# Regrouping the slots of expert weights, moving side loads out of a mixture's head, and waiting for down weights by halves

## The reference

```
def moe_ffn(h, router_w, router_bias, w_gate, w_up, w_down):
    scores = softmax(h @ router_w)                  # 256 tokens, 16 experts
    e_idx = the two best experts of the best of four groups, by scores + router_bias
    wts = scores at e_idx, divided by their sum
    out[token] = sum over its two experts e of
                 wts * ((silu(x @ w_gate[e]) * (x @ w_up[e])) @ w_down[e])

x = layer_norm_2(ALPHA * x + g1 * y, ln_g[i, 0], ln_b[i, 0])
f = moe_ffn(x * (1 + sc2) + sh2, router_w, router_bias, exp_w_gate[i], exp_w_up[i], exp_w_down[i])
x = layer_norm_2(ALPHA * x + g2 * f, ln_g[i, 1], ln_b[i, 1])
```

## Time and profile before

| | |
|---|---|
| Median of 3 runs | 2413.11 us (2412.06 to 2414.28) |
| Span of the profiled execution | 2412.0 us |
| TensorE matmuls busy | 2288.5 us, 95% |
| VectorE busy | 1005.7 us, 42% |
| ScalarE busy | 345.9 us, 14% |
| SP's DMA queue | 691.5 MB, 73.1% of 16 DMA engines |
| Longest chain, by engine | PE 72%, DMA 14%, SP's queue 9%, VectorE 3% |

### The profile page before, as it was taken

One profiled execution on the slowest core, in us unless ns is written; L12 is line 12 of the kernel. 1 busy time (PEld: TensorE's weight loads), 2 busy tenths in 40 slices (PEclk: granted clock), 3 DMA queues, 4 the chain that ended last, 5 costly groups with the idle time before them and its releaser, 6 DMA issues.

```text
span 2412.0 us, 26071 instructions
## 1 busy us (share of the span) xinstructions
PE 2288.5 (95%) x10504; PEld 1393.8 (58%) x10504; DVE 1005.7 (42%) x2156; ACT 345.9 (14%) x705; POOL 54.5 (2%) x98
## 2 busy tenths in 40 slices
PE   6999999999999999999999999888899999998887
PEld 5888698458887785476554443333397544433333
DVE  5265656768666567124643211111235522111112
ACT  2221111001220110011531111111100011111111
POOL 0100000002000000000000000000000000000000
PEclk9999999999999999999999999999999999999999
DMA  9745968856467687532059999999944399999996
GB/s 321 261 174 197 331 229 302 315 195 227 147 255 289 241 300 293 204 115 67 36 215 383 423 421 424 424 423 422 410 172 174 125 388 421 423 424 424 424 421 274
DMA packets 181444, 706.31 MB, mean 293 GB/s; under 512 B 9296, under 2 KB 18768, under 8 KB 153424
## 3 DMA queue, kind: packets, MB, share of 16 engines
q1 hardware_dynamic: 176656, 691.50, 73.1%
q0 software_dynamic: 4672, 13.14, 1.6%
HBM read 699.33 MB, written 5.28 MB: 292 GB/s over the span
## 4 chain that ended last, share of the span: by engine, by line
PE 72%; DMA 14%; SPq 9%; DVE 3%; ACT 1%; issue 1%; DVEq 0%; ACTq 0%
PE banks L624 70%; DMA ring<-in_exp_w_up_dram 6%; DMA acc<-in_exp_w_down_dram 3%; DMA ring<-in_exp_w_down_dram 3%; SPq L2630 3%; SPq L2634 2%; SPq L2663 2%; SPq L2632 2%; DMA arena<-in_exp_w_down_dram 1%; DMA ring<-in_w_ada_dram 1%; DVE acc L1826 0%; PE banks L686 0%; DVE acc L1799 0%; ACT arena L1651 0%; ACT UT L1459 0%
## 5 line engine op out<-in xcount | busy, mean ns | idle before, releaser
L624 PE MATMUL banks<-ring,arena 128*64 128x512 f32 (+2 forms) x2624 | 718.7, 589 | 41.2 <-DMA ring<-in_exp_w_up_dram 21.4
L624 PE MATMUL banks<-UT,ring 128*128 128x256 f32 (+1 forms) x3696 | 728.6, 356 | 8.9 <-ACT UT L1459 4.3
L624 PEld LDWEIGHTS banks<-UT,ring 128*128 128x128 f32 x3696 | 623.7, 193 | 87.0 <-issue 13.6
L624 PEld LDWEIGHTS banks<-ring,arena 128*64 128x64 f32 (+1 forms) x2624 | 290.1, 151 | 439.3 <-issue 406.0
L624 PE MATMUL banks<-arena 128*64 128x512 f32 (+5 forms) x1220 | 239.0, 493 | 13.3 <-DMA acc<-in_exp_w_down_dram 5.6
L1826 DVE SCALAR_TENSOR_TENSOR acc<-ring,cact,acc 128x512 f32<-128x512 f32 x280 | 212.7, 760 | 9.9
L2231 DVE TENSOR_TENSOR arena<-arena,banks 128x512 f32<-128x512 f32 x32 | 34.0, 1062 | 416.9 <-PE banks L624 416.9
L624 PEld LDWEIGHTS banks<-arena 128*64 128x64 f32 (+2 forms) x1220 | 100.2, 158 | 134.3 <-issue 119.8
L1623 ACT ACTIVATE arena<-banks 128x512 f32<-128x512 f32 (+1 forms) x96 | 65.3, 680 | 782.7 <-PE banks L624 743.5
L2239 DVE TENSOR_TENSOR arena<-banks,acc 128x512 f32<-128x512 f32 x32 | 22.1, 692 | 208.8 <-PE banks L624 208.8
L624 PE MATMUL banks<-ring,XN 128*128 128x512 f32 (+1 forms) x192 | 73.1, 540 | 2.8 <-DVE XN L1996 2.8
(11 more groups left out here) (262 smaller groups left out, 1690.3 us busy)
## 6 DMA issues: line engine op xcount, KB each, us to landing
ring<-in_exp_w_gate_dram SPq DMA_DIRECT2D x40, 2048.0 KB, 26.0
ring<-in_exp_w_up_dram SPq DMA_DIRECT2D x40, 2048.0 KB, 25.0
ring<-in_exp_w_down_dram SPq DMA_DIRECT2D x40, 2048.0 KB, 27.8
ring<-in_w_in_dram SPq DMA_DIRECT2D x26, 2048.0 KB, 14.0
ring<-in_mod_w_dram SPq DMA_DIRECT2D x24, 2048.0 KB, 9.1
ring<-in_w_ada_dram SPq DMA_DIRECT2D x20, 2048.0 KB, 8.1
ring<-in_w_up_dram SPq DMA_DIRECT2D x16, 2048.0 KB, 9.5
ring<-in_w_down_dram SPq DMA_DIRECT2D x16, 2048.0 KB, 9.7
```

The source lines that it names most:

```text
L624: return nc.tensor.matmul(o, lhs, rhs, start=start, stop=stop)
```

## The change

- The four spare slots are put together anew, by when the buffers die. Slot 6 is now the tables, `diag` and trig, slot 7 one stretch of the arena, slot 8 XN and two stretches of the arena, slot 9 UT, `grow` and parts of acc and the arena. `PARTS` goes from (1, 4, 2, 4) to (4, 1, 3, 4). Some small buffers move out of the way (`GT`, `EQ`, and the hyena's `hid_tmp`, now `wtmp`).
- Three spare pieces are issued ahead of the flag, not two (`EARLY`). The first, slot 6, has a place of its own in the list (`table_piece`): in layer 2 before ring piece 1, with a wait for the last row maximum and the last readers of `diag` and trig; in layer 3 before the spectra. Ring piece 2 of layer 2 is issued ahead of pieces 0 and 1.
- The second gate row is no longer loaded to `grow` in the grouped form, nor waited for, and the norm rows for the end of layers 2 and 3 are loaded by SP behind the last expert's weights (`late_norm_rows`).
- The down product waits for piece 4, then for piece 5. The last expert's piece 5 is loaded in four row blocks with a semaphore each.

The diff, cut to its core:

```diff
-PARTS = (1, 4, 2, 4)
+EARLY = SLOTS + 3
+PARTS = (4, 1, 3, 4)
...
         odd = [
-            [(0, 2, XN[:, :, :]), (2, 1, view(4608, D)), (3, 0, trig[:, :, :].rearrange("p a n -> p (a n)")), (3, 1, acc[:, 1, :])],
-            [(0, 2, UT[:, :, :].rearrange("p (a c) n -> p a (c n)", a=2)), (2, 2, rows2[:, :, :])],
-            [(0, 2, pair(tables[:, 0:2 * D])), (2, 1, view(6016, D)), (3, 0, tables[:, 2 * D:2 * D + 512]), (3, 1, view(7040, 512))]]
+            [(0, 2, None, tables[:, 0:2 * D].rearrange("p (a n) -> p a n", n=D)), (2, 1, None, diag),
+             (3, 1, 0, tables[:, 2 * D:2 * D + 512]), (3, 1, 1, trig[:, :, :].rearrange("p a n -> p (a n)"))],
+            [(0, 4, None, view(0, 4, D))],
+            [(0, 2, None, XN[:, :, :]), (2, 1, None, view(4608, D)), (3, 1, None, view(6016, D))],
+            [(0, 2, None, UT[:, :, :].rearrange("p (a c) n -> p a (c n)", a=2)), (2, 1, None, grow),
+             (3, 1, 0, acc[:, 1, :]), (3, 1, 1, view(7040, 512))]]
...
-                        w = [slot(4 + h, e) for h in range(2)]
                         bank = start("down", e)
                         for h in range(2):
+                            w = slot(4 + h, e)
                             for j in range(4):
+                                if e == NE - 1 and h == 1 and j:
+                                    pe.wait_ge(m["late_full"][j], 16)
...
-                dve.wait_ge(grow_loaded, 16 * (2 * L + 2))
                 dve.wait_ge(gsplit_loaded, 32 * (L - 1))
...
-                G.dma_start(grow[:, :], gate_rows[n].partition_broadcast(P)).then_inc(grow_loaded, 16)
-                if L >= 2 and i:
+                if L < 2 or i == 0:
+                    G.dma_start(grow[:, :], gate_rows[n].partition_broadcast(P)).then_inc(grow_loaded, 16)
+                else:
...
-                load_lnrow(2 * L + 1)
+                if L < 2:
+                    load_lnrow(2 * L + 1)
                 gate_row(L, 1)
...
+            def table_piece(L):
+                if L == 2:
+                    sp.wait_ge(max_ready, UNIT_BASE[2] + 2 * PAIRS)
+                    for g in (("rmsrow", 1), ("ff", 1, 1, 1, 1)):
+                        filled(sp, g)
+                else:
+                    sp.wait_ge(*read(2, WIDE * ((6 * NE - SLOTS - 1) // WIDE) + SLOTS))
+                load_spare(L, 0, 1, 0)
+
             def spare_pieces(L):
                 sp.wait_ge(*released[("wo", L, 1)])
-                for k in range(2):
-                    load_spare(L, k, 1, k)
+                for i in range(1, EARLY - SLOTS):
+                    load_spare(L, i, 1, i)
+
+            def late_norm_rows(L):
+                sp.wait_ge(x_ready, 2 * (2 * L + 1))
+                for i, row in enumerate((a["ln_g_2"], a["ln_b_2"])):
+                    sp.dma_start(lnrow[:, i, :], row[L - 2, 1].partition_broadcast(P)).then_inc(late_rows_loaded, 16)
...
-                    for i in range(SLOTS + 2, 6 * NE):
+                    for i in range(EARLY, 6 * NE):
                         e, k = divmod(i, 6)
                         s = i % WIDE
                         if i >= WIDE:
                             sp.wait_ge(*read(L, i - WIDE))
-                        elif i == SLOTS + 2:
-                            sp.wait_ge(grow_loaded, 16 * (2 * L + 2))
                         if s >= SLOTS:
                             load_spare(L, k, e, s - SLOTS)
+                        elif i == 6 * NE - 1:
+                            dst = ring[:, s, :].rearrange("p (k n) -> p k n", n=D)
+                            sp.dma_start(dst[:, 0], expert(L, k)[:, e, 0]).then_inc(slot_full[s], 16)
+                            for r in range(1, 4):
+                                sp.dma_start(dst[:, r], expert(L, k)[:, e, r]).then_inc(m["late_full"][r], 16)
...
+            order = list(pieces)
+            order.remove(("moe", 2, 2))
+            order.insert(order.index(("moe", 2, 0)), ("moe", 2, 2))
```

More of the change, by code:

```diff
@@ L364, in build @@
         ftm = acc
-        hid_tmp = view(6144, 2, 512)
         ZT = XN
@@ L461, in build @@
                 d_silu=sem(f"dense_silu{L}"), spare_full=[sem(f"spare_slot_full{L}{i}") for i in range(4)],
-                d_late=[sem(f"dense_late_full{L}{k}") for k in range(SLOTS)], half_read=sem(f"first_half_read{L}"),
+                late_full=[sem(f"late_fill{L}{k}") for k in range(SLOTS)], half_read=sem(f"first_half_read{L}"),
                 onehot=sem(f"onehot_ready{L}"), scaled=sem(f"gather_scaled{L}"), pw=sem(f"scatter_weights_ready{L}"))
@@ L1039, in slot @@
                         pe.wait_ge(m["spare_full"][i], 16 * PARTS[i] * (turn + 1))
-                        return odd[i - 1] if i else spare
+                        return odd[i]
                     _, use = place[("moe", L, s)]
@@ L1048, in half_row @@
                         return w[:, kk, cols]
[L1049 to L1054, removed]
+                    for k0, n, half, v in w:
+                        if k0 <= kk < k0 + n and half in (None, h):
+                            return v if half is not None else v[:, cols] if n == 1 else v[:, kk - k0, cols]
                 def grouped():
@@ L1906, in finish_tiles @@
             def finish_tiles(name, gate, tmp, k, plain=None, between=None):
-                dve.wait_ge(grow_loaded, 16 * (2 * gate[0] + gate[1] + 1))
+                dve.wait_ge(grow_loaded, 16 * (min(2 * gate[0], gate[0] + 2) + gate[1] + 1))
                 for t in range(TT):
@@ L2241, in dense @@
                 def dense():
-                    dve.wait_ge(m["spare_full"][0], 16)
+                    for i in range(EARLY - SLOTS):
+                        dve.wait_ge(m["spare_full"][i], 16 * PARTS[i])
                     V.memset(ACC, 0.0).then_inc(m["pw"], 1)
@@ L2684, in _ @@
             occupant = {}
-            for key in pieces:
+            order = list(pieces)
+            order.remove(("moe", 2, 2))
+            order.insert(order.index(("moe", 2, 0)), ("moe", 2, 2))
+            for key in order:
                 kind, l, j = key
@@ L2692, in _ @@
                     sp.dma_start(rbias[:, :], a["router_bias_2"].partition_broadcast(P)).then_inc(rest_loaded, 16)
-                if key in (("moe", 2, 0), ("moe", 2, 3)):
-                    store_spectrum(j // 3)
+                if key in (("moe", 2, 2), ("moe", 2, 3)):
+                    store_spectrum(j - 2)
+                if key in (("moe", 2, 1), ("spec", 0, 0)):
+                    table_piece(2 if kind == "moe" else 3)
                 if s in occupant and kind != "stage":
@@ L2720, in _ @@
                         other_experts(l)
+                        late_norm_rows(l)
                         for k in range(SLOTS):
```

38 lines of the change are left out of this document (20 added, 18 removed).

## The result

| | before | changed |
|---|---|---|
| Median (lowest to highest) | 2412.59 us (2409.45 to 2414.28) | 2398.28 us (2396.72 to 2399.80) |
| Ratio, with 95% interval | | 0.9935 (0.9923 to 0.9947) |
| Span of the profiled execution | 2412.0 us | 2397.5 us |

The account below looks back on a forecast made before the run. The queue of transfers, not TensorE, was taken to end each mixture. Heads (6.5 + 5.5) and tails (1.1 + 1.0) sum to 14.1 us, giving a span of 2397.9 and a median of 2399.0, range 2392 to 2406.

Parts of the forecast that it names:

- Where the bound lies: Both mixtures: the queue of transfers ends each, not TensorE; earlier transfers gain only what they take from its continuous part.
- The head: Start of each mixture: piece 14 flows earlier, by 6.5 us in layer 2 and 5.5 us in layer 3.
- the cold start: Head of each mixture, pieces issued into an empty queue: starting it costs 1.5 us, bounds 1.1 and 2.7.
- the rate of the full queue: Continuous stretch of each mixture: nine more transfers a layer and three for the split piece cost 0.
- the backlogs of the prediction's sums: Kernel before, at the issue of piece 14: transfers lag by 8.0 us in layer 2, 7.0 us in layer 3.
- about half is lost again in waiting for slots: Mixture heads: of 12 us promised by an earlier piece (4.96) and the removed wait (7.1), about half is lost.
- The tail: Last expert's down product, waiting for its pieces separately: halves give 1.1 and 1.0 us, not 7.1.
- Costs taken as nothing: Norm rows hidden by 7 us, first hyena pieces by 4 us, added transfers in the loop taken as 0.
- the rival of 0.5 to 1%: Weaker case: new parts or cold starts slow the stream, 4 to 8 us over 164 pieces; 2403 to 2407; 8%.
- The sum: Whole kernel: 6.5 + 5.5 + 1.1 + 1.0 = 14.1 us, span 2397.9, median 2399.0.
- the series rival: Each added transfer costs its start in series, 24 x 1.5 = 36 us, less 14.1: 2435; 5%.
- The rival with no slot limit: Mixture heads: the whole early start reaches the end, 12.7 and 12.0 us; with the tail 26.8, 2386.3; 5%.

Follow-up runs that it names:

- Window nine: Changed kernel with a window of nine slots, SP waiting from piece 10 on for the read of piece i - 9: 2411.78 us, ratio 0.9990.
- each half of the change alone: Kernel before without gate row load and wait: 2405.51 us, 0.9969; changed kernel with that load, wait and POOL's norm rows restored: 2403.16 us, 0.9952.
- the last two experiments: Changed kernel plus slot 4's half signal, last expert's gather, scatter, transposes before up: 2395.36 us, 0.9915; same, scatter between gate's halves: 2391.72 us, 0.9910.

## Why the prediction was right, by its steps

**Where the bound lies: right.** The distances to the last up half fell by what the queue gained, and nothing upstream of it mattered (table piece, norm rows). Window nine's 4.8 us per piece is the most direct sign.

**The head: mechanism right, size 1.2 us too high.** 6.5 and 5.5 were forecast, 6.17 and 4.58 came (within the bounds, 5.3 to 6.9 and 4.3 to 5.9). Pieces 14 and 15 left where they were expected, and the cold start cost 1.6 us by bytes in both layers, where 1.5 was taken. The term that was off is the one taken as nothing, the rate of the full queue, which took 0.4 and 0.6 us. From the backlogs of the prediction's sums that leaves 8.0 - 1.6 - 0.4 = 6.0 and 7.0 - 1.6 - 0.6 = 4.8 us, within 0.2 of 6.17 and 4.58. The experiments bear out "about half is lost again in waiting for slots": each half of the change alone gives nearly the whole, and an earlier slot gives the 3.2 us that an earlier issue could not.

**The tail: right.** 1.1 and 1.0 forecast, 1.14 and 1.03 measured as B's gain less A's, 1.1 and 1.4 by undoing it. Gather, scatter, transposes and the copy are late next, as said; shortening that chain in the last two experiments gave 1.0 to 2.2 us more.

**Costs taken as nothing: right but for one.** Norm rows and the hyena's first pieces (its first product waits for ScalarE, 1.31 us, and not for weights) cost nothing that shows. The new slots with their twelve extra transfers a layer cost 0.1 to 0.2% of the rate, 1.0 us in both layers together. That is small beside the rival of 0.5 to 1%, but it is most of what the head fell short by (12.0 forecast, 10.75 measured).

**The sum.** 12.9 us of the 14.4 are the change's (6.17 + 4.58 + 1.14 + 1.03), against 14.1 forecast. The other 1.5 (2.20 - 0.68) lie outside the mixtures: C varies from 206.2 to 208.5 us over the kernels of the experiments, which all do the same work there. So the forecast came within 0.7 us of the median partly by luck; its own terms together were 1.2 too high.

**The rules and rivals weighed.** The Trainium skill, page DMA: Bandwidth & Descriptors, section Bandwidth, asks for batches of at least 1 MiB. This trace agrees only faintly: with 18 transfers to ten pieces in place of 17, the added ones of 0.26 to 0.5 MB, the full queue goes from 423 to 422 GB/s. By the 0.4 and 0.6 us above that is at most 0.05 us for each added transfer, and a start of 1.6 us is paid only where the queue was empty, so the series rival (2435) falls. The rival with no slot limit (2386.3) needed 12.7 and 12.0 us at the head and falls by the 6.17 and 4.58 that came.

## What to carry to other kernels

- When the queue of transfers is the bound, an earlier issue gains only until the next thing that holds the queue. Find which read frees the slot that comes next, and put a signal at that read's half: here that one signal gave 3.2 us more in each layer, where one more early piece (4.96 us) and a wait of 7 us removed had given 6.2 and 4.6 together.
- Two edits that remove the same delay don't add. Price each alone and both together before crediting either.
- Count from one event to another within an execution. Medians of the same kernel moved by 2.9 us, these distances by 0.4.
- Check a cost that was taken as nothing in windows of the same length and place before and after. A rate lower by 0.1% is easily missed, and over 400 us it was the largest error of this forecast at the head.

## What the runs showed of the hardware

**TensorE's clock fell briefly in both kernels, and not alike.** At the start of the hyena mixer behind layer 2, TensorE has done 16 small products, 2.62 us of nothing, eight transposes (1.06 us) and a wait of 1.31 us. Then 96 products begin, and through the first of them the granted clock is at its lower level (0.50, 1.2 of 2.4 GHz); it returns to 1.00 after a time that varies. Windows of the changed kernel, whose 96 products begin at 1742.93 (the granted clock is the number ahead of the DMA share):

```profile
1744.00:1746.00 2.00, 2.00 (x11) 2.00 (x11) 1.45 (x2) 0.36 (x2) 0.00 (x0) 0.50 1.02 376
1746.00:1748.00 2.00, 2.00 (x19) 2.00 (x18) 0.00 (x0) 0.00 (x0) 1.76 (x4) 0.92 1.05 387
```

Windows of the kernel with the norm rows on POOL's queue, whose products begin at 1744.86:

```profile
1746.00:1748.00 2.00, 2.00 (x12) 2.00 (x11) 1.45 (x2) 0.29 (x2) 0.00 (x0) 0.50 1.03 382
1748.00:1750.00 2.00, 2.00 (x11) 2.00 (x11) 0.00 (x0) 0.00 (x0) 1.83 (x4) 0.50 1.06 388
```

The same 96 products take 12.57 us in the one, 13.84 in the other, and 13.98 in the kernel before. Over the profiles of this study they fall into two groups, 12.4 to 12.7 us and 13.4 to 14.0, and eight transposes ahead of layer 3's routing (1.23 us in the changed kernel, 1.98 at clock 0.50 in the kernel before) do the same in the same kernels. (13.98 - 12.57) + (1.98 - 1.23) = 2.16 us is nearly all of C's 2.20. Kernels with the same code at this place stand in both groups, so the edit does not set it directly; what does is open.

**An empty queue restarts slowly, a full one hardly notices a transfer more.** The restart at piece 14 moved 66, 180, 311 and 459 KB in its first four microseconds, against 423 in each when full, and lost 1.6 us in both layers. In the full queue twelve more transfers and new slots together lost 0.4 and 0.6 us over 402 us.
